# RMS norms of a fused two-block decoder kernel: sums in token strips on TensorE, spread by products, and GpSimd's share moved to VectorE

## The reference

```python
def rms_norm(x, g):
    xf = x.astype(F32)
    y = xf * lax.rsqrt(jnp.mean(xf * xf, axis=-1, keepdims=True) + EPS)
    return (y * g.astype(F32)).astype(x.dtype)
...
    x = x + rms_norm(mix, mix_norm_post[l])
    h = rms_norm(x, mem_norm_pre[l])
    m = rms_norm(mem, mem_norm_kv[l])
    x = x + rms_norm(memory_attention(h, m, w_mq[l], w_mk[l], w_mv[l], w_mo[l]), mem_norm_post[l])
    h = rms_norm(x, ffn_norm_pre[l])
    x = x + rms_norm(conv_ffn(h, w_up[l], conv_w[l], conv_b[l], w_down[l]), ffn_norm_post[l])
...
    for i in range(DEPTH_2):
        u = _rmsnorm(h, norm_w[i])
        ...
            h = h + _short_conv_mixer(u, conv_in_w[j], conv_w[j], conv_out_w[j])
        ...
            h = h + _mlstm_mixer(u, mlstm_in_w[j], mlstm_gate_b[j], mlstm_head_norm_w[j], mlstm_out_w[j])
    h = _rmsnorm(h, final_norm_w)
```

## Time and profile before

| | us |
|---|---|
| median of 3 runs (1011.34 to 1011.88) | 1011.6 |
| the profiled execution | 1010.35 |
| its span, first to last instruction | 1008.6 |
| TensorE busy | 973.9 |
| VectorE busy | 689.5 |
| ScalarE busy | 583.3 |
| GpSimd busy | 162.6 |
| TensorE clock granted, mean | 0.991 |

### The profile page before, as it was taken

The page is one execution under the profiler, slowest core; times in us unless marked ns, Lnnn a source line. Parts: engine busy times, 40 slices in busy tenths (PEclk is TensorE's granted clock), DMA queues, the critical chain, the costliest instruction groups (busy, mean ns, idle before and its releaser), DMA issues. The chain is left out here.

```text
span 1008.6 us, 20207 instructions
## 1 busy us (share of the span) xinstructions
PE 973.9 (97%) x7493; PEld 932.5 (92%) x7493; DVE 689.5 (68%) x1038; ACT 583.3 (58%) x868; POOL 162.6 (16%) x167
## 2 busy tenths in 40 slices
PE   7999989999999999999999999999999999999997
PEld 6997769899899999998999999999999999999986
DVE  5888765654698887546877777766666447668843
ACT  6468455646488876554656666654563426654643
POOL 4003003201334445013111111101110000000000
PEclk9999989999999999999999999999999999999999
DMA  7653314434255555662555555565456443234551
GB/s 270 229 164 125 106 64 168 133 119 152 78 181 181 182 187 186 221 198 84 167 169 176 174 168 166 170 196 175 155 166 200 131 145 122 88 128 166 184 174 60
DMA packets 45173, 159.01 MB, mean 158 GB/s; under 512 B 6035, under 2 KB 7059, under 8 KB 44860
## 3 DMA queue, kind: packets, MB, share of 16 engines
q1 hardware_dynamic: 44668, 156.61, 47.3%
q0 software_dynamic: 448, 1.59, 0.5%
HBM read 157.11 MB, written 1.06 MB: 157 GB/s over the span
## 5 line engine op out<-in xcount | busy, mean ns | idle before, releaser
L1453 DVE TENSOR_TENSOR w_lo<-raw,w_hi 128x1024 fp32r<-128x1024 f32 x290 | 358.9, 1243 | 137.8 <-ACT w_hi L540 137.3
L540 ACT ACTIVATE w_hi<-raw 128x1024 fp32r<-128x1024 f32 x290 | 302.6, 1053 | 101.6 <-PE acc L1001 68.2
L999 PE MATMUL acc<-XH,w_hi 128*128 128x272 f32 (+1 forms) x1104 | 320.1, 290 | 10.6 <-DVE XL L1477 4.9
L1001 PE MATMUL acc<-XH,w_lo 128*128 128x272 f32 (+1 forms) x1104 | 316.8, 287 | 0.0
L1000 PE MATMUL acc<-XL,w_hi 128*128 128x272 f32 (+1 forms) x1104 | 316.0, 286 | 0.0
L999 PE MATMUL acc<-AH,w_hi 128*128 128x256 f32 (+1 forms) x832 | 239.6, 288 | 0.9 <-DVE AL L1472 0.9
L1001 PE MATMUL acc<-AH,w_lo 128*128 128x256 f32 (+1 forms) x832 | 236.9, 285 | 0.0
L1000 PE MATMUL acc<-AL,w_hi 128*128 128x256 f32 (+1 forms) x832 | 236.6, 284 | 0.0
L999 PEld LDWEIGHTS acc<-XH,w_hi 128*128 128x128 f32 x1104 | 209.6, 190 | 14.2 <-issue 10.9
L1000 PEld LDWEIGHTS acc<-XL,w_hi 128*128 128x128 f32 x1104 | 209.6, 190 | 0.2
L1001 PEld LDWEIGHTS acc<-XH,w_lo 128*128 128x128 f32 x1104 | 209.8, 190 | 0.0
(11 more groups left out here) (348 smaller groups left out, 1314.9 us busy)
## 6 DMA issues: line engine op xcount, KB each, us to landing
raw<-weights SPq DMA_DIRECT2D x290, 512.0 KB, 3.6
cst<-params SPq DMA_DIRECT2D x1, 1195.0 KB, 12.3
XR<-x_t SPq DMA_DIRECT2D x2, 512.0 KB, 4.5
Y<-mem_t SPq DMA_DIRECT2D x1, 1024.0 KB, 9.8
AR<-bias_rows POOLq DMA_DIRECT2D x1, 1024.0 KB, 8.5
out<-AR SPq DMA_DIRECT2D x2, 512.0 KB, 3.0
AR<-final_gain POOLq DMA_DIRECT2D x1, 512.0 KB, 3.5
AR<-onehot SPq DMA_DIRECT2D x1, 66.0 KB
```

The lines of the kernel that those rows point to most:

```text
L540: nc.scalar.activation(w_hi[:, n % SLOTS, :], raw[:, n % SLOTS, :], ACT.Copy).then_inc(hi_ready, 1)
L999: nc.tensor.matmul(acc(t)[:, 0:w], wh, xh(k), start=(k0 == 0 and k == order[0]), stop=False)
L1001: last = nc.tensor.matmul(acc(t)[:, 0:w], wl, xh(k), start=False, stop=(k0 + nk == total and k == order[-1]))
L1453: V.tensor_tensor(w_lo[:, s, :], raw[:, s, :], w_hi[:, s, :].bitcast(F32), ALU.subtract).then_inc(lo_ready, 1)
```

## The change

**Sums in strips.** `sum_strips` makes of one product with 128 x 256 results four: strip r takes the tokens r x 64 to r x 64 + 63 and writes them to the 32 partitions from 32 r. The sum is thus 128 x 64 with each token's value on 32 partitions, and root and reciprocal work on 64 columns (68 for 272 tokens). Then `spread_rstd` brings it to all partitions: four products with a matrix that picks partition 32 r (`pick`), into `outs0` (`spread(w)`, PSUM). VectorE reads this row from PSUM when it scales Y; for the evacuations ScalarE copies it to `rstd` (`keep_rstd`).

**GpSimd out of the norms.** `sum_pairs` is gone: TensorE sums the squares of all 8 tiles in strips (32 products a norm). The tiles 6 and 7 of a join and the odd residues at the start are VectorE's. GpSimd keeps `sum_squares`, the FFN's and the convolution's products and the residues before mLSTM.

**Order at a join.** VectorE interleaves: scale a pair, residues of the pair before, add. ScalarE: XH of a pair, then its squares. The first two chunks of `up` and `conv_in` run side by side by input tile, the third and fourth go to two halves of the bank `scores`, and the sum of X's squares stands in the middle of the third chunk, the spread in that of the fourth. In front of memory attention the sum stands ahead of `mq`. Keep-warm products are 4 ahead of the spread and 10 after it instead of 28, and 12 more at the start. Weight conversions (`ahead`) move to where an engine would wait.

```diff
+            def sum_strips(src, w, start, stop, bank=OB[1]):
+                w //= STRIPS
+                for r in range(STRIPS):
+                    last = nc.tensor.matmul(bank[r * STRIP:(r + 1) * STRIP, 0:w], ones_d[:, 0:STRIP], src[:, r * w:(r + 1) * w],
+                                            start=start, stop=stop)
+                return last
+            def spread_rstd(e, w, dst=None):
+                pe.wait_ge(inverted, e + 1)
+                dst = spread(w) if dst is None else dst
+                w //= STRIPS
+                for r in range(STRIPS):
+                    last = nc.tensor.matmul(dst[:, span(r, w)], pick[:, r:r + 1].to_broadcast([P, P]),
+                                            root[:, 0:w], start=True, stop=True)
+                last.then_inc(rstd_spread, 1)
             def stat_x(e, count, w):
-                for k in range(0, KT, 2):
-                    pe.wait_ge(pair_summed, 4 * count + k // 2 + 1)
-                    last = nc.tensor.matmul(OB[1][:, 0:w], ones_d[:, :], SQ[:, k, T - w:T], start=(k == 0), stop=(k == KT - 2))
+                for k in range(KT):
+                    if k % 2 == 0:
+                        pe.wait_ge(sq_ready, KT * count + k + 2)
+                    last = sum_strips(SQ[:, k, T - w:T], w, k == 0, k == KT - 1)
...
+            def side_by_side(n, t, o, xh, xl, ready):
+                for c in range(2):
+                    begin(n + c, t + c, True)
+                for k in range(KT):
+                    ready(k)
+                    for c in range(2):
+                        last = three(o(c), n + c, k, xh(k), xl(k), k == 0, k == KT - 1)
...
             stat_y(NORM_MEMOUT, 2)
             keep_warm(WARM)
+            spread_rstd(NORM_MEMOUT, S)
+            keep_warm(WARM_SPREAD)
+            side_by_side(CHUNK["up"], TILE["up"], up_acc, xh, xl, raw_ready(RAW_X2))
+            ffn_pe(0, 2, lambda: stat_x(NORM_X2, 2, S))
+            ffn_pe(0, 3, lambda: spread_rstd(NORM_X2, S))
...
+            stat_x(NORM_X1, 1, S)
             for m in range(KT):
-                chunk(CHUNK["mq"] + m, TILE["mq"] + m, xh, xl, S, ready=raw_ready(RAW_X1) if m == 0 else None)
-                if m == 0:
-                    stat_x(NORM_X1, 1, S)
+                chunk(CHUNK["mq"] + m, TILE["mq"] + m, xh, xl, S, ready=raw_ready(RAW_X1) if m == 0 else None,
+                      between=(lambda: spread_rstd(NORM_X1, S)) if m == 0 else None)
...
-                for k in range(0, POOL_FROM, 2):
+                def scale(k):
                     chain.note(V.tensor_tensor(Y[:, k:k + 2, META:T], Y[:, k:k + 2, META:T],
-                                               rstd[:, META:T].unsqueeze(1).to_broadcast([P, 2, S]), ALU.mult))
...
+                scale(0)
+                add(0, update, scaled)
+                for k in range(2, KT, 2):
+                    scale(k)
+                    raw_rest(update, gain, a, k - 2)
+                    raw_rest(update, gain, a, k - 1)
+                    add(k, update, scaled)
```

More of the change, by code:

```diff
@@ L807, in ffn_act @@
                     n, t = CHUNK["up"] + 2 * p + v, TILE["up"] + 2 * p + v
-                    ahead(n, i)
+                    if hidden is not None:
+                        ahead(n, i)
                     wait_evacuated(act, t, i)
@@ L1054, in _ @@
             for k in range(KT):
-                last = nc.tensor.matmul(PTB[:, 0:S], ones_d[:, :], KTm[:, k, :], start=(k == 0), stop=(k == KT - 1))
+                last = sum_strips(KTm[:, k, :], S, k == 0, k == KT - 1, PTB)
             last.then_inc(stat_ready, 1)
@@ L1503, in _ @@
             dve.wait_ge(gains_loaded, 16)
-            reciprocal_root(NORM_X, META)
-            for k in range(KT + 1):
-                apply_norm(PRE_X, "g_mix_pre", META, *raw_parts(META), k)
+            invert_root(NORM_X, S)
+            wait_spread(NORM_X)
+            for k in range(KT + 2):
+                apply_norm(PRE_X, "g_mix_pre", META, spread(S), *raw_parts(META), k)
             lo(1)
@@ L1559, in _ @@
             ahead(n + 3)
-            dve.wait_ge(root_ready, 2)
-            chain.link(V.reciprocal(rstd_m[:, 0:S], root_m[:, 0:S]))
             for j in range(2):
@@ L1811, in ffn_dve @@
                         ffn_taps(p - 1, 1, i)
-                    ahead(n, i)
+                    if not first:
+                        ahead(n, i)
             def ffn_taps(p, v, i):
@@ L1868, in _ @@
             dve.wait_ge(squared_rstd, 1)
-            with dve.Fori(0, E_TILES) as i:
+            conv_dve(0, first=True)
+            chain.count -= 4
+            with dve.Fori(1, E_TILES) as i:
                 chain.begin_round(i, 4)
```

287 lines of the change are left out of this document (162 added, 125 removed).

## The result

The changed kernel takes **1002.18 us** in the median of its runs (1001.27 to 1003.42), the kernel before 1011.74 in the same comparison (1011.34 to 1012.74): ratio 0.9905, 95% interval 0.9888 to 0.9922, so 9.6 us faster. The forecast was 1003.5 with a range of 998.8 to 1010.0. The profiled execution took 1002.0 us with a span of 1000.3, against 1010.35 and 1008.6; 1002.2 had been forecast for it.

The account below looks back on a forecast made before the run. TensorE, busy 97%, was taken as the bound, with stalls at the joins. FFN -2.1, convolution -3.55, memory attention -1.75, start -1.15, mLSTM +0.4 gave -8.15 us: 1002.2 profiled, 1003.5 median with 1.25 added; range 998.8 to 1010.0.

Parts of the forecast that it names:

- Strips, 28 ns a record: Strip sums: 64 records at 28 ns, twice the lower end, so one full sum takes S = 1.8 us.
- The lower end of S: Time S of one full strip sum: at least 0.9 us, from 14 ns a record, a quarter of 58.
- The give-back before the sixth chunk: After the joins: w_lo late behind evacuations and taps on VectorE, losing 0.8 us before the FFN, 0.75 before the convolution.
- The memory norm, -0.5: Memory norm, within the start term: a sum of 3.26 us becomes sum plus spread of 2.75, 0.5 us saved.
- Chain and pace: Join before FFN: first product 5.8 us after `mo`, both chunks done 13.3 after, a pair every 2.0, spread 0.94.
- The slow clock, 1.1 of the 4.3 before the convolution: Join before convolution: the fourth chunk ends 4.3 us earlier, about 1.1 of it from the slow clock going away.
- Memory attention: Join before memory attention: earlier scaling and interleaved chain start the third chunk at 188.8 instead of 190.57, net -1.75 us.
- mLSTM: Join before mLSTM: 16 strip records and the spread replace a 0.72 us sum, +0.4 us with no wait removed.
- 58 ns a record: Rival: strip records don't overlap beyond what the trace shows, S = 3.7, gain 0.5, time about 1011; chance 0.16.
- The serial one, 118 ns a record: Rival: strips run one after the other at a full product's price, S = 7.5, time 1026; chance 0.09, with everything slower.
- The catch-up costs more: Rival: after both large joins a second and third chunk also wait, another 1.5 us a join, 1006.5; chance 0.17.
- S = 0.9: Rival that more is gained: a full strip sum takes 0.9 us or nothing is given back, 999.9; chance 0.16.

Follow-up runs that it names:

- before_pool_out: Kernel before, with tiles 6 and 7 of a join scaled and added by VectorE as a fourth pair, GpSimd keeping the sums: 1006.56 us, ratio 0.9958.
- strips_in_series: Changed kernel, with the same four sums run strip by strip, all 8 tiles into one strip before the next: 1009.0 us.
- full_sums: Changed kernel, with sums as full products again, root and reciprocal on 256 columns in SBUF, no spread and no copy: 1004.67 us.
- pool_beside: Changed kernel, with GpSimd making eight unused additions at the joins before memory attention, FFN and convolution: 1007.58 us.
- one_by_one: Changed kernel, with the first two chunks of up and conv_in computed one after the other, not side by side: 1010.78 us.

## Why the prediction held, and where it did not

- *What bounds the kernel, and the joins*: right. Nothing moved outside them; the last stretch is the same within 0.2.
- *Strips, 28 ns a record*: twice too much. Measured were 14 ns, 0.88 us from first to last record, and 1.22 us a sum with the steps in and out instead of 1.8: 0.6 less at each of three places. By the prediction's own sum, in which S counts four times, that alone would have made the time 1001.1; other terms took it back.
- *The lower end of S*: right by luck. It was a quarter of the 58 ns in the earlier trace rows, read as the price of two halves side by side. Lines 1115 to 1118 of the kernel before write four records in a row to the same half, so that row does not show halves that share time.
- *The give-back before the sixth chunk*: 0.8 forecast, 1.6 at the sixth `up` chunk and 2.0 by the eighth; VectorE's queue was right, its two waits for ScalarE (0.34 and 0.37) were missing. Before the convolution 0.75 forecast, 1.0 at the sixth and 1.2 in the end; there the cause was right: w_lo at 479.43 stands behind the taps. It takes 1.67 us instead of 1.22; GpSimd multiplies beside it from 479.24 to 480.02.
- *The memory norm, -0.5*: not found. The shorter sum ran into the wait for weights that I had said I could not shift; the changed kernel's TensorE, and ScalarE, which waits for a transfer:

```profile
44.69 0.36 PE L1028 MATMUL acc<-XH,w_hi 128*128 128x256 f32 x1 [1.46 <-issue]
```
```profile
42.27 1.06 ACT L547 ACTIVATE w_hi<-raw 128x1024 fp32r<-128x1024 f32 x1 [3.73 <-DMA raw<-weights]
```

From the sum's first record to the product that stands at 56.76 before, 18.93 us pass before and 19.55 now (18.94 and 19.35 in the second traces): 0.4 to 0.6 longer instead of 0.5 shorter.

- *Chain and pace*: 5.75 and 13.4 us for 5.8 and 13.3; a pair every 2.06 us for 2.0; spread 0.98 for 0.94. These were worked out from durations of the same instructions in the profile and came within 0.1.
- *The slow clock, 1.1 of the 4.3 before the convolution*: too much. `before_pool_out` saves 1.05 us of the first chunk with the full clock, and 0.4 of it arrives; the rest was covered by GpSimd's pair sums.
- *Memory attention*: with 1.22 for the sum, 0.6 more than forecast; -2.4 measured, as the mechanism says.
- *mLSTM*: +0.1 instead of +0.4. At the last product ahead of the next wait for VectorE it is +0.24 (27.58 us after the join's start instead of 27.34), and less behind later waits.
- *Rivals*: 58 ns a record would have been right in kind had the strips been ordered otherwise (`strips_in_series`: 47 ns, S about 3.0). The serial one, 118 ns a record, is near neither order. "The catch-up costs more" was true in part, and hidden in the median by "S = 0.9".
- *The range*: the time lies in it, and the gain in the traces, 8.3 us, is nearly the 8.15 forecast. That nearness is partly luck: -1.8 on three sums and -0.3 before mLSTM met +1.2 and +0.5 of give-back, +0.3 in the first stretch and some 0.2 in the first four `conv_in` chunks. The 1.3 us between 1003.5 and the median are of another kind: I had added 1.25 for the distance of before's median from its profiled execution, and in the changed kernel that distance is 0.2.

## What to carry to other kernels

When a sum over partitions stands on the critical path, split its columns over four strips of 32 output partitions and order the products so that neighbours write to different strips; in the other order the same records took 47 ns each instead of 14. Keep GpSimd quiet while VectorE is on the critical path, or let VectorE read one input from PSUM, as the scalings did here (0.69 us beside GpSimd). And when a join gets shorter, look at what each converting engine had in its queue at that moment, table loads included, and at where one of them waits for another: the next late thing may be made up of both.

## What the runs showed of the hardware that I had not expected

- Records of 32 output partitions by 64 columns start 14 ns apart when neighbouring products write to different strips (the changed kernel), 47 ns when they write to the same one (`strips_in_series`).
- A plain float32 record of 128 x 256 takes 216 ns (`full_sums`) where the records of a chunk take 118.
- In `pool_beside` VectorE's scaling with one input in PSUM takes 0.68 or 0.69 us beside a working GpSimd; additions and residues with both in SBUF take 1.6 to 1.8 times as long (1.07 to 1.10 for 0.68, 1.61 for two instead of 0.89).
- In `one_by_one` TensorE stood 1.03 us ahead of the second 6 records and again ahead of the third 6, and the granted clock fell to 0.51; in the changed kernel it stood 0.3 to 0.6 us ahead of every 12 and the clock stayed full. In the kernel before, the clock fell after a single stand of 2.46 us before the convolution and not after one of 2.45 before the FFN; after one of 1.54 (`before_pool_out`) it stayed full.
